# Router logits computed at the end of the merge stage, a scan for the running count, and the slot table built in quarters

## The chip, the cores and the metric

One core of one Trainium2 chip runs the whole kernel. The metric is device time in microseconds (us) of one execution; lower is better.

## The reference

One layer of a hybrid encoder, on x of 2048 tokens x 1024, in float32:

```python
proj = x @ w_in                       # q, k, v of both mixers and the gates
oa   = swa_sink_attention(...)        # 8 heads of 64, window of two 64-token chunks
ob   = diff_attention(...)            # 4 heads, block-causal, then RMSNorm per head
ga, gb = split(sigmoid(gpre + b_gate))
mix = (ga * (oa @ w_proj_a) + gb * (ob @ w_proj_b)) @ w_out
x1  = layer_norm(ALPHA * x + mix)
# mixture of experts: best group of 4, then the best 2 of its 8 experts
glog = x1 @ w_group + b_group         # 4 logits a token
elog = x1 @ w_router + b_router       # 32 logits a token, the chosen group's 8 are kept
eid, wts = top 2 of softmax(elog of the group), scaled by the group's probability
order = argsort(eid)                  # the tokens, sorted by expert
ys  = silu(xs @ gate) * (xs @ up) @ down, expert by expert
out = layer_norm(ALPHA * x1 + scattered sum of wts * ys)
```

## The kernel before, in words

P is 128; the 2048 tokens are NT = 16 tiles of 128 rows. The program is a row of phases (project, diff attention, window attention, merge, route, expert, final). Each phase has a block with one instruction stream per engine, ordered by semaphores alone, and ends with a barrier of all engines. A float32 product is made in three passes of TensorE (PE) from a high part, which ScalarE (ACT) rounds, and a low part, which VectorE (DVE) makes by subtraction.

**Merge** (`merge_phase`, L1368). For each tile PE turns (transposes) `oin` (oa and ob), multiplies by w_proj_a and w_proj_b into the PSUM tiles `psa` and `psb`, turns the gated sum `pa` into `pt`, and multiplies it by w_out into `psw` (L1468 to L1470, 48 matmuls). The order of the work is written out by hand in `step(t, k, u)`: in step t the products of tile t run beside the w_out product of tile t - 1 and the layer norm of tile t - 2. `norm` (L1597) is DVE's: y from `psw`, statistics, a root on ACT, and the scaling; GpSimd (POOL) multiplies by gamma and adds beta, but for the last tile, where DVE does both (L1615, L1617). ACT issues the stores of y to `x1` and to `acc` (L1538, L1539) and at the end waits for them. In the last steps PE has only tile 15's turning and its w_out product left; `psw` is one buffer, so that product waits for `y_done` of tile 14.

**Route** (`route_phase`, L1644). SyncE (SP) loads the router's weights and the 16 tiles of `x1` into four buffers `xin`, and then the 12 slices of expert 0's weights into `rw_raw`. Per tile PE turns the rows (L1767) into one half of `pt`, ACT makes `th` (L1832), DVE makes `tl` (L1869); every fourth tile PE makes the logits of four tiles in 15 matmuls (L1777, L1781), ACT copies them (L1826), PE folds the two halves (L1791) and DVE adds the bias into `lg` (L1863). PE's order is written out by `turn`, `folds`, `logits_of`: a batch's logits come after the turning of the next batch. Then DVE works down one chain, each step `link`ed to the one before by the semaphore `chain`: group and expert choices (L1892 to L1907), the one-hot `o1`, `o2` (L1909), their sum `both` (L1911), its running sum over the tiles in 16 adds (L1913); PE counts with `tri` and `ones` in float32 (L1805 to L1807); DVE does the pair weights (L1919 to L1927), the counts and slots (L1930 to L1947). Last it inverts the permutation: `here` (L1952) and `rows` (L1957) are one-hot comparisons, the four `values` are `here` times the tile (POOL, L1751), times the lane and the low weight (ACT, L1844, L1846) and times the high weight (DVE, L1958), and PE multiplies `rows` by `values` into `table` (L1814, 32 matmuls), from which `weight` and `idx` are read (L1962 to L1969).

**Expert** (`expert_phase`) starts when `idx` stands: ACT and DVE split expert 0's weights (L2170, L2227), POOL gathers the first rows, and PE works through the experts; **final** does the last layer norm.

Of the kernel before, what the change touches and what calls it, by code (L numbers as in the profile page):

```python
# [21 lines left out]
P = 128  # L22
SEQ = 2048
# [78 lines left out]
def f(ap):  # L102

    return ap.bitcast(F32)
# [419 lines left out]
def window_attention_phase(nc, sinks, ident, qk_hi, qk_lo, v_hi, v_lo, oa, w_slices, w_hi, w_lo):  # L524
# [14 lines left out]
    with Phase(nc, "a") as ph:  # L539
# [18 lines left out]
        mask_f = ph.sb("mask_f", [P, P + 2 * M])  # L558
# [93 lines left out]
        def _(pool):  # L652
# [3 lines left out]
            nc.gpsimd.memset(mask_f[:], 0.0).then_inc(mask_step, 1)  # L656
# [134 lines left out]
        def _(dve):  # L791
            dve.wait_ge(mask_step, 10)
            nc.vector.tensor_copy(mask[:], mask_f[:]).then_inc(mask_step, 1)
# [574 lines left out]
def merge_phase(nc, ident, w_hi, w_lo, oa, ob, gates, x, subln_g, ln_g, ln_b, x1, acc):  # L1368
# [4 lines left out]
    KA, KB = A_Q // P, B_V // P  # L1373
    with Phase(nc, "m") as ph:
# [15 lines left out]
        sd, rs = ph.sb("sd", [P, 1]), ph.sb("rs", [P, 1])  # L1390
        pt = ph.ps("pt", [P, D])
# [11 lines left out]
        out_step, stored = ph.sem("out_step"), ph.sems("stored", 2)  # L1403
        block = ph.block()

# [15 lines left out]
        def _(sp):  # L1421
# [31 lines left out]
            for src, dst in ((ln_g, gam), (ln_b, bet)):  # L1453
                sp.dma_start(dst[:], src.to_broadcast([P, D])).then_inc(vec_in, 16)
            over_steps(sp, step)

        @block.tensor
        def _(pe):
# [5 lines left out]
            def product(out, hi, lo, ks, w0, done):  # L1464
                for k in ks:
                    for j in range(D // BANK):
                        js, at, kw = slice(j * BANK, (j + 1) * BANK), slice(k * P, (k + 1) * P), w0 + k
                        nc.tensor.matmul(out[:, js], hi[:, at], w_hi[:, kw, js], start=(k == ks[0]), stop=False)  # L1468
                        nc.tensor.matmul(out[:, js], lo[:, at], w_hi[:, kw, js], start=False, stop=False)
                        last = nc.tensor.matmul(out[:, js], hi[:, at], w_lo[:, kw, js], start=False, stop=(k == ks[-1]))  # L1470
                last.then_inc(done, 1)

            def step(t, k, u):
# [9 lines left out]
                if is_tile(t):  # L1483
# [15 lines left out]
                if is_tile(t - 1):  # L1499
# [9 lines left out]
            over_steps(pe, step)  # L1509

        @block.scalar
        def _(act):
# [12 lines left out]
            def step(t, k, u):  # L1525
# [10 lines left out]
                if is_tile(t - 2):  # L1536
                    act.wait_ge(affine, t - 1)
                    act.dma_start(x1[bass.ts(t - 2, P), :], y[:, u, :]).then_inc(stored[u], 16)  # L1538
                    act.dma_start(acc[bass.ts(t - 2, P), :], y[:, u, :]).then_inc(stored[u], 16)  # L1539

# [5 lines left out]
            over_steps(act, step)  # L1546
            for u in range(2):
                act.wait_ge(stored[u], 32 * (NT // 2 + 1))

        @block.gpsimd  # L1550
        def _(pool):
            nc.gpsimd.memset(eps[:], EPS).then_inc(vec_step, 1)
            nc.gpsimd.memset(eps_x[:], EPS / (ALPHA * ALPHA)).then_inc(vec_step, 1)
            pool.wait_ge(vec_in, 32)
# [14 lines left out]
        def _(dve):  # L1569
# [27 lines left out]
            def norm(t, k, u):  # L1597
# [10 lines left out]
                nc.vector.bn_aggr(mv[:], st[:]).then_inc(var_done, 1)  # L1608
                dve.wait_ge(sd_done, t + 1)
# [833 lines left out]
```

## Time and profile before

| | us |
|---|---|
| median of 3 runs | 2854.07 |
| lowest and highest | 2850.42, 2859.87 |
| the profiled execution | 2856.11 |
| its span | 2854.4 |
| last matmul of the merge ends | 1767.6 |
| first instruction of route | 1778.85 |
| last logits read by DVE | 1831.28 |
| `idx` written | 1870.70 |

| engine | busy us | share of the span |
|---|---|---|
| PE | 2605.3 | 91% |
| DVE | 1629.1 | 57% |
| ACT | 1193.0 | 42% |
| POOL | 530.9 | 19% |

Times inside the execution count from the start of its span. The span and the execution's time differ by 1.7 us that lie around it. The shares are means over stages with different limits; the change touches only the stretch from about 1751 to 1871 us, in which PE's share is far below its mean.

### The profile page before, as it was taken

How to read it: one execution, taken by the hardware profiler on the slowest of the kernel's cores; microseconds unless marked ns; L12 is line 12 of the kernel's file. 1: busy time of each engine (PE TensorE's matmuls, PEld its weight loads, DVE VectorE, ACT ScalarE, POOL GpSimd, SP SyncE). 2: the span in 40 equal slices, each digit the busy share in tenths (PEclk: the TensorE clock that was granted, in tenths of full speed). 3: DMA queues.
4: the chain of work that ended last, by engine and by line, in shares of the span. 5: the costliest groups of instructions: out<-in, count | busy, mean ns of one | idle time of the engine just before them, and what ended most of it. 6: DMA issues, size and time to landing. Idle time of an engine off the chain costs nothing. (4 is left out here: it accounts for less than half of the span.)

```text
span 2854.4 us, 45509 instructions
## 1 busy us (share of the span) xinstructions
PE 2605.3 (91%) x14634; PEld 2245.1 (79%) x14635; DVE 1629.1 (57%) x3067; ACT 1193.0 (42%) x2016; POOL 530.9 (19%) x538
## 2 busy tenths in 40 slices
PE   6999996999999999899799997579999999999990
PEld 5888885788888888799588885468888888888880
DVE  6323322666666666479344443568575577557845
ACT  3111111445444454357111110258575576556846
POOL 0111111101001010135133333022222222222220
PEclk9999998999999999979899998889999999999995
DMA  6344444756575564297333332559687788768946
GB/s 224 122 155 139 136 158 147 215 189 207 168 216 170 178 211 141 94 214 201 134 133 132 132 125 79 211 177 380 233 304 266 235 274 308 233 227 315 379 129 257
DMA packets 262019, 567.45 MB, mean 199 GB/s; under 512 B 27056, under 2 KB 119984, under 8 KB 259872
## 3 DMA queue, kind: packets, MB, share of 16 engines
q1 hardware_dynamic: 169904, 429.45, 44.2%
q0 software_dynamic: 18720, 64.96, 8.8%
q10 hardware_dynamic: 73296, 71.77, 7.4%
q8 instruction: 56, 0.92, 0.1%
q14 instruction: 43, 0.35, 0.0%
HBM read 434.50 MB, written 131.60 MB: 198 GB/s over the span
## 5 line engine op out<-in xcount | busy, mean ns | idle before, releaser
L2227 DVE TENSOR_TENSOR e_wl<-rw_raw,e_wh 128x1024 fp32r<-128x1024 f32 (+1 forms) x384 | 449.6, 1221 | 18.2 <-ACT e_wh L2170 14.4
L2170 ACT ACTIVATE e_wh<-rw_raw 128x1024 fp32r<-128x1024 f32 (+1 forms) x384 | 380.6, 1053 | 4.8 <-PEq L76 4.8
L246 PE MATMUL j_pg<-qkv_w_hi,j_xh 128*128 128x512 f32 (+1 forms) x640 | 243.6, 381 | 10.0 <-DVE qkv_w_lo L416 9.9
L248 PE MATMUL j_pg<-qkv_w_lo,j_xh 128*128 128x512 f32 (+1 forms) x640 | 238.1, 372 | 0.0
L247 PE MATMUL j_pg<-qkv_w_hi,j_xl 128*128 128x512 f32 (+1 forms) x640 | 237.2, 371 | 0.0
L2119 PE MATMUL e_p_up<-e_wh,e_xh 128*128 128x256 f32 (+1 forms) x784 | 225.8, 288 | 0.0
L2121 PE MATMUL e_p_up<-e_wl,e_xh 128*128 128x256 f32 (+1 forms) x784 | 222.0, 283 | 0.0
L2120 PE MATMUL e_p_up<-e_wh,e_xl 128*128 128x256 f32 (+1 forms) x784 | 222.0, 283 | 0.0
L1136 PE MATMUL b_pg<-b_g_wh,b_g_xh 128*128 128x512 f32 x512 | 208.2, 407 | 0.7 <-DVE b_g_out L1323 0.7
L1136 PE MATMUL b_pg<-b_g_wl,b_g_xh 128*128 128x512 f32 x512 | 204.7, 400 | 0.0
L1193 ACT ACTIVATE b_th<-b_t 128x512 fp32r<-128x512 f32 (+3 forms) x160 | 85.4, 534 | 285.0 <-PE b_t L1121 276.3
L1136 PE MATMUL b_pg<-b_g_wh,b_g_xl 128*128 128x512 f32 x512 | 203.1, 397 | 0.0
L1267 DVE TENSOR_SCALAR_CACHE_REDUCE b_sc<-b_s 128x512 f32<-128x512 f32 (+3 forms) x320 | 179.3, 606 | 30.4 <-PE b_s L1108 18.6
L2131 PE MATMUL e_py<-e_wh,e_hh 128*128 128x512 f32 x392 | 166.9, 426 | 0.5
L1308 DVE TENSOR_TENSOR b_tl<-b_t,b_th 128x512 fp32r<-128x512 f32 (+3 forms) x160 | 97.6, 610 | 118.8 <-ACT b_th L1193 118.8
L445 DVE TENSOR_TENSOR j_by_cos<-j_pg,qkv_cos 128x512 f32<-128x512 f32 x64 | 37.7, 589 | 216.4 <-DMA v_lo<-j_staged 145.7
L2119 PE MATMUL e_p_gate<-e_wh,e_xh 128*128 (+1 forms) x392 | 157.2, 401 | 1.3 <-issue 1.3
L1186 ACT ACTIVATE b_sc<-b_sc,b_nb 128x128 f32<-128x128 f32 (+15 forms) x128 | 153.1, 1196 | 6.9 <-DVE b_nb L1278 6.9
L2133 PE MATMUL e_py<-e_wl,e_hh 128*128 128x512 f32 x392 | 154.8, 395 | 0.0
L2132 PE MATMUL e_py<-e_wh,e_hl 128*128 128x512 f32 x392 | 153.9, 393 | 0.0
L2120 PE MATMUL e_p_gate<-e_wh,e_xl 128*128 (+1 forms) x392 | 153.9, 392 | 0.0
L2121 PE MATMUL e_p_gate<-e_wl,e_xh 128*128 (+1 forms) x392 | 153.8, 392 | 0.0
(333 smaller groups left out, 6634.4 us busy)
## 6 DMA issues: line engine op xcount, KB each, us to landing
rw_raw<-w_gate_up SPq DMA_DIRECT2D x256, 512.0 KB, 7.4
rw_raw<-w_down SPq DMA_DIRECT2D x128, 512.0 KB, 9.4
b_g_xh<-xt_hi SPq DMA_DIRECT2D x64, 512.0 KB, 3.7
b_g_xl<-xt_lo SPq DMA_DIRECT2D x64, 512.0 KB, 4.8
gates<-b_g_out ACTq DMA_DIRECT2D x64, 256.0 KB, 5.3
m_gt<-gates SPq DMA_DIRECT2D x16, 1024.0 KB, 8.2
qk_hi<-j_staged ACTq DMA_DIRECT2D x16, 832.0 KB, 4.5
qk_lo<-j_staged ACTq DMA_DIRECT2D x16, 832.0 KB, 7.0
```

What stands on the lines that cost most here:

```text
L246: nc.tensor.matmul(out, xh[:, u, ks], w_hi[:, k, cs], start=(k == 0), stop=False)
L247: nc.tensor.matmul(out, xl[:, u, ks], w_hi[:, k, cs], start=False, stop=False)
L248: last = nc.tensor.matmul(out, xh[:, u, ks], w_lo[:, k, cs], start=False, stop=(k == KD - 1))
L1136: last = nc.tensor.matmul(pg[:], x_side, w_side, start=(q == 0), stop=(q == PASSES - 1))
L1267: nc.vector.tensor_scalar(sc[u][:, m, ks], bank[n % 4][:, 0:ks.stop - ks.start], 1.0, NEG, ALU.mult, ALU.max, accum_out=mx[:, u, m, g:g + ...
L2119: nc.tensor.matmul(out[:, 0:js.stop - js.start], xh[:, at], hi, start=(k == 0), stop=False)
L2120: nc.tensor.matmul(out[:, 0:js.stop - js.start], xl[:, at], hi, start=False, stop=False)
L2121: last = nc.tensor.matmul(out[:, 0:js.stop - js.start], xh[:, at], lo, start=False, stop=(k == KD - 1))
L2131: nc.tensor.matmul(py[:, js], hh[:, at], wh[:, n, js], start=(k == 0), stop=False)
L2133: last = nc.tensor.matmul(py[:, js], hh[:, at], wl[:, n, js], start=False, stop=(k == KF - 1))
L2170: nc.scalar.activation(wh[:, slot(e, s), :], raw[:, s:s + 1, :], ACT.Copy).then_inc(w_hi, 1)
L2227: nc.vector.tensor_tensor(wl[:, slot(e, s), :], raw[:, s:s + 1, :], f(wh[:, slot(e, s), :]), ALU.subtract).then_inc(w_lo, 1)
```

## The change

1. The logits move from the route phase to the end of the merge phase. The landing buffers are `oin` and `gt` (six rows), the turned rows lie in `psa`, `psb` and `pt` in turn, the high and low parts in the first slices of `w_hi` and `w_lo` (w_proj_a's and w_proj_b's place), the copied logits in `pa`. Tiles 0 to 13 are read back from `x1`; 14 and 15 are taken from `y`. Rows 0 and 1 are turned before tile 15's w_out product, row 2 in its middle, the rest after it. SP issues the last two stores instead of ACT. The router's weights are loaded at the merge's start and split in its step 1.
2. In route, the 16 adds become one scan over (expert, tile), which restarts at each expert (`same` is 0 at tile 0); `tri` is shifted by -1 to take the own tile off again; both matmuls go in one pass (float32r), after the column totals; o1 and o2 are made behind the scan. SP loads expert 0's weights first.
3. The table has three values (token, high weight, low weight) instead of four, POOL makes none, and comparison, multiplication and matmuls go by quarters (8 tiles each).
4. `mask_f` of the window attention lies in `raw`.

The core of the diff:

```diff
@@ merge_phase, SP, after over_steps(sp, step)
+            def reload(r):
+                if r < 2:
+                    sp.wait_ge(ab_turned, NT - 1 + r)
+                elif r < len(land):
+                    sp.wait_ge(gated_b, NT - 1 + (r - 2) // 2)
+                else:
+                    sp.wait_ge(r_turned, r - len(land) + 1)
+                sp.wait_ge(stored[r % 2], 32 * (r // 2 + 2))
+                sp.dma_start(land[r % len(land)], x1[bass.ts(r, P), :]).then_inc(landed[r % len(land)], 16)
...
+            for r in range(8):
+                reload(r)
+            store(NT - 2)
+            for r in range(8, FROM_DRAM):
+                reload(r)
+            store(NT - 1)
@@ PE
+                if r < 2:
+                    pe.wait_ge(gated_b if r else gated_a, NT)
+                elif r > 2:
+                    pe.wait_ge(r_lo, r - 2)
+                for c in range(KD):
+                    last = nc.tensor.transpose(buf[:, c * P:(c + 1) * P], src[:, c * P:(c + 1) * P], ident[:])
...
+            def logits_of(i):
+                w = i % 2
+                pe.wait_ge(r_lo, B * i + B)
...
+                if isinstance(t, int) and t == NT:
+                    turn_row(0)
+                    turn_row(1)
...
+                if isinstance(t, int) and t == NT:
+                    pe.wait_ge(y_done, t - 1)
+                    part(psw, mh, ml, range(0, KD // 2), KA + KB, 0, KD - 1)
+                    turn_row(2)
+                    part(psw, mh, ml, range(KD // 2, KD), KA + KB, 0, KD - 1).then_inc(w_done, 1)
...
+            for r in range(3, 6):
+                turn_row(r)
+            logits_of(0)
+            for i in range(1, NBATCH):
+                for r in range(4 * i + 2, min(4 * i + 6, NT) if i < NBATCH - 1 else NT):
+                    if r == 4 * i + 4:
+                        folds(i - 1)
+                        logits_of(i)
+                    turn_row(r)
+            folds(NBATCH - 2)
+            logits_of(NBATCH - 1)
+            folds(NBATCH - 1)
@@ DVE, in norm, between the statistics and the root's reciprocal
+                if isinstance(t, int) and t == NT - 1:
+                    low_row(3)
@@ route_phase, POOL
-                nc.gpsimd.tensor_tensor(values[:, c, :, 0, :], here[:, c], tile_f[:].unsqueeze(2).to_broadcast([P, NT, SLOTS]),
-                                        ALU.mult).then_inc(tiled, 1)
@@ PE
+            nc.tensor.matmul(pc[:], ones_r[:], upto[:, :, NT - 1], start=True, stop=True).then_inc(product, 1)
+            nc.tensor.matmul(pp[:].rearrange("p e t -> p (e t)"), tri_r[:], both[:].rearrange("p e t -> p (e t)"), start=True, stop=False)
+            nc.tensor.matmul(pp[:].rearrange("p e t -> p (e t)"), ones_r[:], upto[:].rearrange("p e t -> p (e t)"), start=False, stop=True).then_inc(product, 1)
@@ DVE
+            link(tt(either[:], sel1[:], sel2[:], ALU.add))
+            link(tt(both[:].rearrange("p (g e) t -> p t g e", g=NG), either[:].unsqueeze(2).to_broadcast([P, NT, NG, EPG]), gate4, ALU.mult))
+            nc.vector.tensor_tensor_scan(upto[:].rearrange("p e t -> p (e t)"), same[:].rearrange("p e t -> p (e t)"),
+                                         f(both[:]).rearrange("p e t -> p (e t)"), 0.0, ALU.mult, ALU.add).then_inc(counted, 1)
...
-            for t in range(NT):
-                ins = tt(before[:, t + 1, :], before[:, t, :], both[:, t].rearrange("p g e -> p (g e)"), ALU.add)
...
-            link(tt(place[:], pp[:], base[:].unsqueeze(1).to_broadcast([P, NT, NE]), ALU.add))
+            dve.wait_ge(product, 2)
+            link(tt(place[:], pp[:].rearrange("p e t -> p t e"), base[:].unsqueeze(1).to_broadcast([P, NT, NE]), ALU.add))
...
+            for c, ts_of in QUARTERS:
+                n = ts_of.stop - ts_of.start
+                tt(rows[:, c, ts_of], ...)
+                dve.wait_ge(in_tile, c + 1)
+                tt(values[:, c, ts_of, 0, :], here[:, c, ts_of], token_f[:, ts_of].unsqueeze(2).to_broadcast([P, n, SLOTS]), ALU.mult)
+                tt(values[:, c, ts_of, 1, :], here[:, c, ts_of], f(pair_hi[:, c, ts_of]).unsqueeze(2).to_broadcast([P, n, SLOTS]),
+                   ALU.mult).then_inc(valued, 1)
```

How the order moves, first on PE at the merge's last tile. Before, tile 15's turning is followed at once by its w_out product:

```order
L1470 MATMUL m_psw<-mw_w_lo,m_mh 128x512
L1461 MATMUL m_pt<-ident,m_pa 128x128 x8
L1468 MATMUL m_psw<-mw_w_hi,m_mh 128x512
L1469 MATMUL m_psw<-mw_w_hi,m_ml 128x512
L1470 MATMUL m_psw<-mw_w_lo,m_mh 128x512
```

and in the changed kernel:

```order
L1520 MATMUL m_psw<-mw_w_lo,m_mh 128x512
L1511 MATMUL m_pt<-ident,m_pa 128x128 x8
L1543 MATMUL m_psa<-ident,m_oin 128x128 x8
L1543 MATMUL m_psb<-ident,m_oin 128x128 x8
L1518 MATMUL m_psw<-mw_w_hi,m_mh 128x512
L1519 MATMUL m_psw<-mw_w_hi,m_ml 128x512
L1520 MATMUL m_psw<-mw_w_lo,m_mh 128x512
```

The turnings of rows 0 and 1 (L1543) stand between the two.

DVE at the end of the merge, from tile 15's statistics on. Before:

```order
L1608 BN_AGGR m_mv<-m_st 128x2
L1610 RECIPROCAL m_rs<-m_sd 128x1
L1615 SCALAR_TENSOR_TENSOR m_y<-m_y,m_mv,m_gam 128x1024
L1617 SCALAR_TENSOR_TENSOR m_y<-m_y,m_rs,m_bet 128x1024
L72 UNCONDITIONAL_BRANCH
```

and in the changed kernel, where L1778 makes a row's low part and L1783 reads logits:

```order
L1760 BN_AGGR m_mv<-m_st 128x2
L1778 TENSOR_TENSOR mw_w_lo<-m_psa,mw_w_hi 128x8x128
L1764 RECIPROCAL m_rs<-m_sd 128x1
L1769 SCALAR_TENSOR_TENSOR m_y<-m_y,m_mv,m_gam 128x1024
L1771 SCALAR_TENSOR_TENSOR m_y<-m_y,m_rs,m_bet 128x1024
L1778 TENSOR_TENSOR mw_w_lo<-m_psb,mw_w_hi 128x8x128
L1778 TENSOR_TENSOR mw_w_lo<-m_pt,mw_w_hi 128x8x128
L1778 TENSOR_TENSOR mw_w_lo<-m_psa,mw_w_hi 128x8x128
L1778 TENSOR_TENSOR mw_w_lo<-m_psb,mw_w_hi 128x8x128
L1783 TENSOR_TENSOR lg<-m_psw,m_br 128x144
```

Row 3 lies inside the last norm, rows 4 to 15 and the four reads behind it.

## Rows read from the trace of the kernel before

**Rows 1.** Stretches: length, busy us of PE, PEld, DVE, ACT, POOL, granted clock, DMA.

```profile
1755.00:1759.00 4.00, 4.00 (x11) 3.17 (x12) 2.22 (x5) 0.29 (x1) 1.15 (x1) 0.60 0.02 4
1768.00:1785.00 17.00, 0.00 (x0) 0.00 (x0) 5.98 (x12) 0.74 (x2) 2.54 (x12) 0.61 0.39 107
1789.00:1799.00 10.00, 5.80 (x44) 4.55 (x43) 7.16 (x6) 5.78 (x6) 0.00 (x0) 1.00 0.87 283
...
1831.00:1833.00 2.00, 0.00 (x0) 0.00 (x0) 1.76 (x9) 0.09 (x1) 0.00 (x0) 1.00 0.03 12
...
1849.00:1864.00 15.00, 0.00 (x0) 0.00 (x0) 14.40 (x20) 6.93 (x23) 5.81 (x2) 0.50 0.00 0
```

**Rows 2.** Timeline of the merge's end: start us, length us, engine.

```profile
1754.86 0.77 PE L1468 MATMUL m_psw<-mw_w_hi,m_mh 128*128 128x512 f32 x1 [3.59 <-DVE m_y L1602]
...
1766.08 0.39 PE L1468 MATMUL m_psw<-mw_w_hi,m_mh 128*128 128x512 f32 x1
1766.76 0.39 PE L1468 MATMUL m_psw<-mw_w_hi,m_mh 128*128 128x512 f32 x1
...
1767.64 1.23 DVE L1602 SCALAR_TENSOR_TENSOR m_y<-m_psw,m_xin 128x1024 f32<-128x1024 f32 x1 [9.87 <-PE m_psw L1470]
...
1772.43 1.28 DVE L1617 SCALAR_TENSOR_TENSOR m_y<-m_y,m_rs,m_bet 128x1024 f32<-128x1024 f32 x1
```

**Rows 3.** Timeline of route's logits: a row's steps, and the last batch.

```profile
1804.43 1.94 ACT L1832 ACTIVATE r_th<-r_pt 128x1024 fp32r<-128x1024 f32 x2 [0.28 <-PE r_pt L1767]
1805.49 2.36 DVE L1869 TENSOR_TENSOR r_tl<-r_pt,r_th 128x1024 fp32r<-128x1024 f32 x2 [3.33 <-ACT r_th L1832]
...
1809.70 0.43 PE L1777 MATMUL r_plt<-r_th,r_wr_hl 128*72 128x512 f32 x1
...
1813.44 1.91 PE L1767 MATMUL r_pt<-ident,r_xin 128*128 128x128 f32 x16
...
1829.20 0.59 ACT L1826 ACTIVATE r_lt<-r_plt 72x512 f32<-72x512 f32 x1 [4.89 <-PE r_plt L1777]
...
1830.97 0.31 DVE L1863 TENSOR_TENSOR r_lg<-r_pl,r_br 128x144 f32<-128x144 f32 x1 [5.18 <-PE r_pl L1791]
```

**Rows 4.** DVE's chain in route, up to the slots.

```profile
1833.66 1.05 DVE L1903 TENSOR_REDUCE r_el<-r_wide 128x128 f32<-128x512 f32 x1
...
1840.59 3.58 DVE L1913 TENSOR_TENSOR r_before<-r_before,r_both 128x32 f32<-128x32 f32 x16
...
1848.31 0.19 DVE L1930 TENSOR_SCALAR r_cnt_f<-r_pc 128x32 f32<-128x32 f32 x1 [2.36 <-PE r_pc L1807]
...
1849.39 0.22 DVE L1935 TENSOR_TENSOR_SCAN r_incl<-r_ones,r_tiles 128x32 f32<-128x32 f32 x1
...
1850.31 0.69 DVE L1940 TENSOR_TENSOR r_place<-r_pp,r_base 128x512 f32<-128x512 f32 x1
```

**Rows 5.** Timeline of the table and of the hand-over to the experts.

```profile
1857.09 4.02 DVE L1957 TENSOR_TENSOR r_th<-r_count_f,r_slot_row 128x2048 fp32r<-128x2048 f32 x1
...
1863.87 2.28 DVE L1957 TENSOR_TENSOR r_th<-r_count_f,r_slot_row 128x2048 fp32r<-128x2048 f32 x1
1864.00 5.58 PE L1814 MATMUL r_pt<-r_tl,r_th 128*128 128x256 f32 x32 [15.73 <-DVE r_tl L1958]
1866.07 1.21 DVE L1958 TENSOR_TENSOR r_tl<-r_xin,r_pair_hi 128x1024 fp32r<-128x1024 f32 x1
1869.63 0.23 DVE L1962 COPY weight<-r_pt 128x64 f32<-128x64 f32 x1 [2.34 <-PE r_pt L1814]
...
1870.42 0.28 DVE L1969 SCALAR_TENSOR_TENSOR idx<-r_empty,r_spare_lane,r_token 128x64 int32<-128x64 f32 x1
1871.65 5.79 ACT L2170 ACTIVATE e_wh<-rw_raw 128x1024 fp32r<-128x1024 f32 x6 [4.76 <-PEq L76]
```

**Rows 6.** The transfers: expert 0's first load, time to landing of `r_xin`.

```profile
1809.97 5.48 SPq L2409 DMA_DIRECT2D rw_raw<-w_gate_up  x8
...
DMA to landing us min/median/max: 3.2/4.5/7.3
```

More of the change, by code:

```diff
@@ L1462, in turn, with part @@
                 last.then_inc(done, 1)
-            def product(out, hi, lo, ks, w0, done):
+            def part(out, hi, lo, ks, w0, first, end):
                 for k in ks:
@@ L1471, in product, with turn_row @@
-                last.then_inc(done, 1)
+                        last = nc.tensor.matmul(out[:, js], hi[:, at], w_lo[:, kw, js], start=False, stop=(k == end))
+                return last
+            def product(out, hi, lo, ks, w0, done):
+                part(out, hi, lo, ks, w0, ks[0], ks[-1]).then_inc(done, 1)
+            def turn_row(r):
+                buf = turned_in[r % 3]
+                if r < FROM_DRAM:
+                    pe.wait_ge(landed[r % len(land)], 16 * (r // len(land) + 1))
+                    src = land[r % len(land)]
+                else:
+                    if r == NT - 1:
+                        pe.wait_ge(last_affine, 1)
+                    else:
+                        pe.wait_ge(affine, r + 1)
+                    src = y[:, r % 2, :]
+                if r < 2:
[4 more added lines that the diff above has]
+                    last = nc.tensor.transpose(buf[:, c * P:(c + 1) * P], src[:, c * P:(c + 1) * P], ident[:])
+                last.then_inc(r_turned, 1)
@@ new lines, in logits_of, with high @@
+            def logits_of(i):
+                w = i % 2
+                pe.wait_ge(r_lo, B * i + B)
+                if i == 0:
+                    pe.wait_ge(wr_split, 2)
+                    pe.wait_ge(y_done, NT)
+                else:
+                    pe.wait_ge(lt_done, i)
+                for c in range(KD):
+                    def high():
+                        return nc.tensor.matmul(plt, wr_hl[:, c, :], th[:, w, c, :], start=(c == 0), stop=(c == KD - 1))
+                    if c == 0:
+                        high()
+                    nc.tensor.matmul(plt[0:NL, :], wr_hl[:, c, 0:NL], tl[:, w, c, :], start=False, stop=False)
+                    if c:
+                        last = high()
+                last.then_inc(r_product, 1)
@@ L1473, in step, with folds @@
+            def folds(i):
+                pe.wait_ge(lt_done, i + 1)
+                if i:
+                    pe.wait_ge(logits, i)
+                else:
+                    pe.wait_ge(fold_step, 3)
+                for v in range(B):
+                    last = nc.tensor.matmul(pl[:, v, :], lt[:, i % 2, v * P:(v + 1) * P], fold[:], start=True, stop=True)
+                last.then_inc(folded, 1)
             def step(t, k, u):
@@ L1697, in route_phase @@
         found, split_pair = ph.sem("found"), ph.sem("split_pair")
         block = ph.block()
[L1704 to L1707 removed]
+        QUARTERS = [(c, slice(n * NT // 2, (n + 1) * NT // 2)) for c in range(2) for n in range(2)]
@@ L1770, in logits_of @@
-            def logits_of(i, w):
-                pe.wait_ge(t_lo, B * i + B + 2)
-                pe.wait_ge(lt_done, i + 1)
-                for c in range(KD):
-                    def high():
-                        return nc.tensor.matmul(plt[:], wr_hl[:, c, :], th[:, w, c, :], start=(c == 0), stop=(c == KD - 1))
-                    if c == 0:
-                        high()
-                    nc.tensor.matmul(plt[0:NL, :], wr_hl[:, c, 0:NL], tl[:, w, c, :], start=False, stop=False)
-                    if c:
-                        last = high()
-                last.then_inc(product, 1)
@@ L1804, in _ @@
[L1804 to L1813 removed]
+            pe.wait_ge(one_pass, 2)
```

295 lines of the change are left out of this document (138 added, 157 removed).

## The prediction

> **What bounds the kernel now.** I read the page first: PE is busy 91% of the span, so only a stretch in which PE waits can give time back at little cost. The busy time by stretches shows where that is: for 17 us around the end of the merge PE does nothing, in route's logits it is busy 5.80 of 10 us, and from 1849 to 1864 us it rests while DVE is busy 14.40 of 15 us [rows 1]. The timeline then gives the chain from the merge's last product to `idx`. The product waits 3.59 us for `psw`, runs at a clock of 0.60 at first, and DVE's norm follows until 1773.7 [rows 1, 2]. The last logits are read at 1831.28 [rows 3]. DVE alone goes on [rows 4], then DVE and PE make the table, and the first expert work follows `idx` by 0.95 us (1870.70 to 1871.65) [rows 5]. Nothing else of the kernel can begin before that, so what leaves this chain leaves the time. After it PE is the bound as before, and the change leaves that part alone.
>
> **A: the logits in the merge's tail.** What it removes: the wait for the stores, the barrier, the loads' latency and the start of route, during which no logits are made.
>
> - Last product. Rows 0 and 1 are turned (0.95 us each, 1.91 for two [rows 3]) in the 3.59 us in which PE waited, at no cost, since y_done of tile 14 still ends later. The product is 16 groups of three matmuls 0.68 apart, 10.9 us at the full clock [rows 2], plus row 2's turning, 0.95. Begun at 1754.86, it ends at 1766.7 instead of 1767.6: I take the clock to stay up, since only 1.7 us stay idle. If it falls as before (0.60), the end is 1768.5.
> - Norm of tile 15. It takes 6.1 us (1767.64 to 1773.71 [rows 2]); row 3's low part (1.2 us) comes in, of which the wait for the root hides 0.4. It ends at 1773.6: nothing gained, nothing lost, and row 3 is done.
> - First logits: PE begins them at row 3's low part, about 1771.1, and they end at 1775.0 (15 matmuls took 3.75 us from 1809.70 to the next turning [rows 3], and the last ends 0.15 later). Rows 6 and 7 are turned behind them and ACT makes row 7's high part by 1777.9 (0.97 a row [rows 3]) and DVE its low part by 1779.3. Logits 1 begin at 1779.4.
> - Batches 2 and 3. The order has the four turnings directly ahead of their own logits, so nothing covers the last row: first row 0.95, the high part 1.1 later (behind ACT's copy), then four low parts at 1.18 (2.36 for two [rows 3]), 0.1 to PE: 6.85 us, and 3.75 us of logits, 10.6 a batch. DVE sets it; in route's order the turnings of the next batch covered that row. Logits 3 begin at 1779.4 + 2 x 10.6 = 1800.6 and end at 1804.5.
> - The end: from the last matmul to the last read took 2.1 us (ACT's copy at 1829.20, read done at 1831.28 [rows 3]), so 1806.6. Then the barrier, for which I take the 0.95 us of the next boundary, and 0.2 for the first `iota`. The stores of tile 15 are long done by then. The chain starts 24.7 - 1.15 = **23.5 us** earlier.
>
> The reloads are hidden: six rows have buffers, a reload has six turnings' time (some 16 us) and lands in 3.2 to 7.3 [rows 6]. SP is held at the store of tile 14 until POOL has added beta, during the last product; reload 8 behind it is first needed near 1783. The early part of the merge gets four small loads, 0.9 us of ACT and DVE, in steps where both idle 10 us: nothing. `mask_f` costs nothing: `raw` is filled after the first scores, which wait for the mask.
>
> **B: counting.** Gone are the 16 adds, 3.5 us, and DVE's wait for PE, 2.36 [rows 4], since o1, o2 and the pair weights now stand between; the sum `both` of 0.69 goes as well. New are `either` (128 elements, 0.3 by the rows for 32 and 512), `both` with a strided output, the scan, and three casts that ran at route's start (0.45 together). For `both` I take the strided reduction's 1.05 rather than 0.69 (same 512 elements [rows 4]), and the same 0.36 more for `place`, which now reads PSUM in strides; the ends are 0 and 0.36 for each. The scan: 0.22 us for 32 elements beside 0.19 for a plain operation of that size, so 0.03 x 16 = 0.5 on top of 0.69 [rows 4], 1.2; the ends are 0.69 and 1.4. Sum: -3.5 - 2.36 - 0.69 + 0.3 + 1.05 + 1.2 + 0.45 + 0.36 = **-3.2**.
>
> The two rows are 0.03 us apart at 32 elements, which could as well be a fixed cost and make the scan 0.7. Here a page speaks against the cheap reading: the Trainium skill, "DVE: opcode table, instruction layouts, handler registers and perf-mode slots", section "Datapath and trigger behaviour", says that the built-in scan runs at half throughput. By it B would be -3.2, by the fixed-cost reading -3.7. On strides, the Trainium skill, "SBUF — State Buffer", section "Door 1: The DMA port swizzle", says that accesses pay for each new 16-byte line, and 8-byte in PSUM; by that the PSUM read could cost more than the 0.36 of the SBUF row, which no row here shows.
>
> **C: the table.** Before: `rows` and `values` on DVE took 10.2 us (1857.09 to 1867.28), of which POOL's work beside them cost some 3.4: the same comparison took 4.02 with POOL busy and 2.28 without [rows 5]. Now a quarter is 1.17 (half of 2.28) and two multiplications of 512 elements, 0.62 each back to back: 2.4, four of them 9.65. **-0.5**. ACT has 8 of its 0.24 us multiplications a quarter, 1.95: hidden. Behind the last DVE instruction PE had 16 matmuls of 256 columns, 2.35 us to the read [rows 5]; now 8 of 192, 1.3 us at the clock of 0.50 that stretch shows [rows 1], plus 0.2: **-0.85**. One DVE step of the read goes: **-0.15**.
>
> **Sum.** -23.5 - 3.2 - 0.5 - 0.85 - 0.15 = -28.2 us. The profiled execution took 2856.1, so 2827.9. It lies 2.0 us over the median of the three runs; for a median I forecast 2826, which is 1.0% less.
>
> **Rivals.**
>
> 1. *The clock falls in the tail.* PE now waits some 2 us for DVE in each batch, and at the merge's end a gap of 3.59 us brought 0.60 for the next 4 us [rows 1, 2]. Against it: with PE busy 58% in route's first turnings the clock stayed at 1.00 [rows 1]. If it fell in all four batches, 15 matmuls would cost 0.2 more each, 3 us a batch, and the exposed turning 0.7: 15 us, so 2841.
> 2. *B and C give nothing* (strides, the scan and the quarters' fixed costs eat it): 23.5 remain, 2830.5. It lies inside the range.
> 3. *Expert 0's weights become the bound.* They were first issued at 1809.97 and the transfers were over by about 1831 [rows 1, 6], 21 us; the first issue is now near 1808, so they stand by 1829, and `idx` is due at 1842.5. The cover is 13 us. Only with twice the duration would the gain shrink, at worst to nothing: 2854. Against it: nothing else loads then.
> 4. *The reloads bind: slower.* Rows 6 to 13 are read back in two rounds, each waiting for a buffer and then for a landing. Beyond 16 us of landing each round costs what lies over it. To eat 28 us and 9 more, a landing would have to take 34 us; the longest of these loads took 7.3 [rows 6]. 2865 if so.
>
> **How the numbers follow.** Forecast with its bounds: 0.85; rival 1: 0.07; rival 2 is part of the forecast's lower gain; rival 3: 0.04; rival 4: 0.02; 0.02 for what I have not seen. The range: a batch of 10.2 to 12 us (-1, +3), the boundary 0.5 to 3 (-0.5, +2), the product's clock (+2), B (-1, +1.5) and the runs' own spread, 2850.4 to 2859.9 (-3, +4). Taken together 2819 to 2834. A measurement of this kernel tells 0.3%, 8.6 us, from no change. Faster by more than that holds for the forecast, rival 1 and 2: 0.93; same 0.04; slower 0.03.
>
> **What would show it right or wrong.** The last read of logits near 1806.6, a batch every 10.6 us, DVE without a gap in the four low parts, the last product ending before 1767 at a clock near 1.0; DVE's scan at 1.2 and no wait for PE at the counts; comparisons of 1.2 us with POOL idle; the read of the table 1.5 us behind the last multiplication; `idx` near 1842.5. A landing over 10 us, or a batch over 12 us, would make the forecast wrong, and so would an expert phase that grows.

## The result, and the profile after

| | us |
|---|---|
| before, median of 4 runs | 2853.02 (2850.42 to 2859.87) |
| the changed kernel, median of 4 runs | 2826.82 (2825.18 to 2831.76) |
| ratio, 95% interval | 0.9908 (0.9895 to 0.9922) |
| the profiled execution, its span | 2831.76, 2830.0 |

By the medians the change is faster by 26.2 us, 0.9%; a median of 2826 was forecast. The profile shows where that comes from. "Turning" is a transpose on PE, and "the tail" is the merge's last stretch, in which PE, ACT and DVE now make the logits. The stretches first, with the columns of [rows 1]:

```profile
1755.00:1759.00 4.00, 4.00 (x13) 3.15 (x12) 3.44 (x6) 2.12 (x3) 1.96 (x1) 0.60 0.22 87
...
1785.00:1795.00 10.00, 7.72 (x45) 5.40 (x44) 4.92 (x5) 3.88 (x4) 0.00 (x0) 0.86 0.00 0
...
1795.00:1807.00 12.00, 9.73 (x56) 6.93 (x55) 4.93 (x5) 4.47 (x5) 0.00 (x0) 0.83 0.01 1
...
1826.00:1828.00 2.00, 0.00 (x0) 0.00 (x0) 1.79 (x8) 0.00 (x0) 0.00 (x0) 0.50 1.06 352
...
1831.00:1846.00 15.00, 8.09 (x32) 7.12 (x32) 12.82 (x22) 7.74 (x32) 0.00 (x0) 0.50 0.00 1
```

PE now works where it had rested, from 1785 to 1807, but in both of these stretches, and at the start of tile 15's product, the granted clock is a mean between 1.2 and 2.4 GHz (0.86, 0.83, 0.60) where I had taken 1.00. (Before, the start of the product was at 0.60 too.) No transfer of note runs from 1785 to 1807. The clock stands at 0.50 while the table is made. PE in the tail, with the wait ahead of each row in brackets, as in [rows 2]:

```profile
1754.05 0.47 PE L1518 MATMUL m_psw<-mw_w_hi,m_mh 128*128 128x512 f32 x1 [1.85 <-DVE m_y L1754]
...
1754.86 0.63 PE L1518 MATMUL m_psw<-mw_w_hi,m_mh 128*128 128x512 f32 x1
...
1790.88 0.45 PE L1557 MATMUL m_psw<-mw_w_hi,m_wr_hl 128*72 128x512 f32 x1 [1.56 <-DVE mw_w_lo L1778]
...
1792.77 0.63 PE L1557 MATMUL m_psw<-mw_w_hi,m_wr_hl 128*72 128x512 f32 x1
...
1796.20 1.03 PE L1543 MATMUL m_psa<-ident,m_oin 128*128 128x128 f32 x8
...
1803.14 0.70 PE L1557 MATMUL m_psw<-mw_w_hi,m_wr_hl 128*72 128x512 f32 x1 [1.56 <-DVE mw_w_lo L1778]
```

After a rest of 1.85 us the product's matmuls go from 0.39 us to 0.63, and after one of 1.56 the third batch of logits does the same. From that batch's first matmul to the first turning behind it pass 5.32 us; the second batch, with its matmuls at 0.39 to 0.40, took 3.77. PE has no wait for a DMA between the merge's last product and the last logits. DVE beside it:

```profile
1767.81 1.23 DVE L1754 SCALAR_TENSOR_TENSOR m_y<-m_psw,m_xin 128x1024 f32<-128x1024 f32 x1 [3.21 <-PE m_psw L1520]
...
1786.07 1.23 DVE L1778 TENSOR_TENSOR mw_w_lo<-m_pt,mw_w_hi 128x1024 fp32r<-128x1024 f32 x1 [5.74 <-ACT mw_w_hi L1673]
1787.21 1.22 DVE L1778 TENSOR_TENSOR mw_w_lo<-m_psa,mw_w_hi 128x1024 fp32r<-128x1024 f32 x1
1788.34 1.22 DVE L1778 TENSOR_TENSOR mw_w_lo<-m_psb,mw_w_hi 128x1024 fp32r<-128x1024 f32 x1
1789.60 1.23 DVE L1778 TENSOR_TENSOR mw_w_lo<-m_pt,mw_w_hi 128x1024 fp32r<-128x1024 f32 x1
1790.74 0.30 DVE L1783 TENSOR_TENSOR lg<-m_psw,m_br 128x144 f32<-128x144 f32 x1
...
1810.13 0.31 DVE L1783 TENSOR_TENSOR lg<-m_psw,m_br 128x144 f32<-128x144 f32 x1 [6.83 <-PE m_psw L1573]
1811.70 0.28 DVE L1944 CAST r_desc<-r_desc_i 128x8 f32<-128x8 int32 x1 [1.26 <-POOL r_desc_i L1881]
1812.02 0.22 DVE L1948 TENSOR_REDUCE r_gm<-lg 128x16 f32<-128x64 f32 x1
```

The four low parts run without a gap, 1.13 to 1.26 apart. The batches follow each other by 10.71 and 12.26 us (1780.17, 1790.88, 1803.14): DVE and the full-clock logits give the first, the slow matmuls the second. A batch is 16 matmuls in the code and in the trace, not the 15 that I counted; the time of a batch was read from the trace and stands. The last logits are read at 1810.44. Behind that, the constants of route are POOL's, and DVE's first reduction starts 1.58 us after the read (0.23 before, 1831.28 to 1831.51). DVE's chain, against [rows 4, 5]:

```profile
1818.92 0.28 DVE L1964 TENSOR_TENSOR r_either<-r_sel 128x128 f32<-128x128 f32 x1
1819.24 1.01 DVE L1965 TENSOR_TENSOR r_both<-r_either,r_gsel 128x512 fp32r<-128x512 f32 x1
1820.29 1.23 DVE L1967 TENSOR_TENSOR_SCAN r_upto<-r_same,r_both 128x512 fp32r<-128x512 f32 x1
...
1825.03 0.18 DVE L1989 TENSOR_SCALAR r_cnt_f<-r_pc 128x32 f32<-128x32 f32 x1
...
1827.04 0.69 DVE L2000 TENSOR_TENSOR r_place<-r_pp,r_base 128x512 f32<-128x512 f32 x1
...
1833.69 1.22 DVE L2015 TENSOR_TENSOR r_rows<-r_count_f,r_slot_row 128x1024 fp32r<-128x1024 f32 x1
1834.82 0.69 DVE L2018 TENSOR_TENSOR r_values<-r_here,r_token_f 128x512 fp32r<-128x512 f32 x1
1835.42 0.69 DVE L2019 TENSOR_TENSOR r_values<-r_here,r_pair_hi 128x512 fp32r<-128x512 f32 x1
...
1842.44 0.68 DVE L2019 TENSOR_TENSOR r_values<-r_here,r_pair_hi 128x512 fp32r<-128x512 f32 x1
1845.24 0.23 DVE L2024 COPY weight<-r_table 128x64 f32<-128x64 f32 x1 [2.11 <-PE r_table L1909]
```

The scan takes 1.23 us, the strided `both` 1.01. `place` reads PSUM in strides in the same 0.69 us as the contiguous one [rows 4]. No wait for PE stands at the counts: the column totals were ready before they were wanted. A quarter's comparison takes 1.22. PE and POOL, up to the first expert's first product:

```profile
1821.66 0.37 PE L1901 MATMUL r_pc<-r_upto,r_ones_r 128*128 128x32 f32 x1 [11.56 <-DVE r_upto L1967]
...
1843.18 2.02 PE L1909 MATMUL r_table<-r_values,r_rows 128*128 128x192 f32 x8 [0.31 <-DVE r_values L2019]
...
1848.05 2.10 POOL L2106 DMA_INDIRECT e_xg<-x,e_idx_in  x1 [0.93 <-POOL e_idx_in L2103]
...
1859.74 0.79 PE L2180 MATMUL e_p_gate<-e_wh,e_xh 128*128 x1 [1.26 <-issue]
```

The counts' first matmul needs 0.37 us and starts behind the scan. Eight table matmuls take 2.02 us, 0.25 each, at the clock of 0.50. The gather's instruction took 2.10 us on POOL here (1.04 before), and PE's first product comes 13.69 us behind `idx` (12.05 before).

### The profile page after: what moved, and what is told of

Its sections match the earlier page's. It is cut to its first block and busy times, and to the rows that moved or that the text cites. A ratio compares the mean times of both kernels' runs of the same rounds, so it can differ in the third digit from the quotient of the medians.

```text
span 2830.0 us, 45509 instructions
## 1 busy us (share of the span) xinstructions
PE 2608.0 (92%) x14631; PEld 2248.3 (79%) x14632; DVE 1625.0 (57%) x3059; ACT 1190.8 (42%) x2016; POOL 527.2 (19%) x538
```

## The experiments

The profiled executions reach the merge's end up to 12 us apart (1744.4 in t1, 1756.3 in t8), and t7, which is the change once more, reaches it 4.7 us before the change's first profile, so the cause lies in earlier phases. Whether the small loads and splits that the change adds ahead of that point cost anything can't be told: its eleven profiles reach it at 1744.4 to 1756.3, the one of before at 1753.5. So I measure each profile from M, where DVE starts to read `psw` for tile 14 (1753.50 before, 1752.69 after). The parts: **product** from M to the same read for tile 15; **logits** on to the end of their last read; **gap** to the first reduction; **counts** to `cnt_f`; **table** to the first read of the table; **to idx** on to the end of `idx`'s writing. All are in us, one profiled execution each.

| kernel | product | logits | gap | counts | table | to idx | M to idx |
|---|---|---|---|---|---|---|---|
| before | 14.14 | 63.64 | 0.23 | 16.80 | 21.32 | 1.07 | 117.20 |
| the change | 15.12 | 42.63 | 1.58 | 13.01 | 20.21 | 0.81 | 93.36 |
| t1 logits only | 13.50 | 45.57 | 3.75 | 16.78 | 22.21 | 1.07 | 102.88 |
| t2 logits, counts | 15.06 | 44.12 | 1.57 | 13.07 | 21.79 | 1.07 | 96.68 |
| t3 PE kept on | 13.47 | 39.78 | 1.58 | 13.00 | 20.21 | 0.81 | 88.85 |
| t4 rows ahead | 13.50 | 36.40 | 1.58 | 13.01 | 20.21 | 0.81 | 85.51 |
| t5 table warm | 13.47 | 41.31 | 1.57 | 13.01 | 20.20 | 0.81 | 90.37 |
| t6 halves | 15.08 | 42.61 | 1.57 | 13.00 | 21.50 | 0.81 | 94.57 |
| t7 the change again | 15.07 | 42.60 | 1.57 | 13.00 | 20.20 | 0.81 | 93.25 |
| t8 all together | 13.46 | 35.00 | 1.57 | 13.00 | 20.21 | 0.81 | 84.05 |
| t9 rows ahead, kept on | 13.46 | 34.96 | 1.58 | 13.01 | 20.21 | 0.81 | 84.03 |
| t10 t4 again | 13.46 | 36.55 | 1.58 | 13.02 | 20.21 | 0.81 | 85.63 |

The times, with the kernel before measured beside them (t1 to t4 ran on one chip, t5 to t8 on a second, t9 and t10 on a third):

| kernel | time | kernel before | ratio, interval |
|---|---|---|---|
| t1 | 2834.78 (2832.83 to 2842.10) | 2853.03 | 0.9942 (0.9919 to 0.9965) |
| t2 | 2826.73 (2822.45 to 2834.13) | 2853.03 | 0.9900 (0.9881 to 0.9920) |
| t3 | 2825.66 (2825.15 to 2826.60) | 2853.03 | 0.9901 (0.9883 to 0.9919) |
| t4 | 2821.43 (2819.39 to 2825.54) | 2853.03 | 0.9892 (0.9872 to 0.9911) |
| t5, t6, t7 | 2830.04, 2831.78, 2825.91, one run each | 2855.66 | |
| t8 | 2822.16 (2820.65 to 2826.66) | 2855.66 | 0.9879 (0.9863 to 0.9896) |
| t9 | 2821.90 (2817.98 to 2831.92) | 2856.51 | 0.9891 (0.9873 to 0.9910) |
| t10 | 2820.32 (2815.46 to 2825.19) | 2856.51 | 0.9877 (0.9860 to 0.9894) |

### t1: the logits alone

The merge is the changed one; route's counting and table are those of before.

```diff
-            nc.vector.tensor_tensor_scan(upto[:].rearrange("p e t -> p (e t)"), same[:].rearrange("p e t -> p (e t)"),
-                                         f(both[:]).rearrange("p e t -> p (e t)"), 0.0, ALU.mult, ALU.add).then_inc(counted, 1)
...
+            for t in range(NT):
+                ins = tt(before[:, t + 1, :], before[:, t, :], both[:, t].rearrange("p g e -> p (g e)"), ALU.add)
...
-            for c, ts_of in QUARTERS:
+            for c in range(2):
```

> Part A alone: the logits are made in the merge's tail as in the change, but the counting (16 adds, float32 matmuls) and the table (four values, POOL makes one) are those of before. My theory, from the two traces: A gives 18.7 us up to the first step of the chain, B 3.8 and C with the read 1.4, so in this kernel DVE's counts begin 16.8 us after the first reduction as before (13.0 in the change), the table takes 21.3 to 21.6 us from there to its read, and the whole is 5 us slower than the change: about 2832 us. Rival: B and C are worth nothing once A moves the work (what they save returns as a wait at the experts' start): then the time is that of the change, 2827.

Measured: 18.3 us less than before and 8 more than t2 and the change, where 5 more than the change was expected; to `idx` it takes 9.5 us more than the change. DVE's rows on the counts and the table, and below them two stretches of before:

```profile
1824.02 0.19 DVE L2002 TENSOR_SCALAR r_cnt_f<-r_pc 128x32 f32<-128x32 f32 x1 [2.37 <-PE r_pc L1916]
...
1846.23 0.23 DVE L2034 COPY weight<-r_pt 128x64 f32<-128x64 f32 x1 [3.22 <-PE r_pt L1923]
```

```profile
1864.00:1865.00 1.00, 1.00 (x4) 1.00 (x5) 1.00 (x1) 1.00 (x6) 0.00 (x0) 0.50 0.00 0
...
1868.00:1869.00 1.00, 1.00 (x11) 1.00 (x10) 0.00 (x0) 0.00 (x0) 0.00 (x0) 1.00 0.00 0
```

The wait for the counts is back with 2.37 us, and the comparison of `rows` takes 4.02 (at 1832.81) beside POOL, as before [rows 4, 5]. Two numbers are new. The gap is 3.75 us and not 1.58, because this route's DVE still waits for all of POOL's constants, the last of them a 0.94 us fill:

```profile
1805.72 0.94 POOL L1905 MEMSET r_zero<- 128x1024 f32 x1
```

So 2.2 us of what I had booked under A are earned by the rewritten start of route, not by the move of the logits. And the table is read 3.22 us behind the last multiplication, where before, with the same 32 matmuls, it was 2.35. What differs is when the clock rises in the middle of them: their starts go from 0.21 us apart to 0.12 at 1867.5 before, for the last 16, and here at 1845.2, for the last 7. The last batch of logits was slow here too, 14 of its 16 matmuls.

### t2: the logits and the counts, the table as before

```diff
-        QUARTERS = [(c, slice(n * NT // 2, (n + 1) * NT // 2)) for c in range(2) for n in range(2)]
+        QUARTERS = [(c, slice(0, NT)) for c in range(2)]
...
+            pool.wait_ge(in_tile, 1)
+            for c in range(2):
+                nc.gpsimd.tensor_tensor(values[:, c, :, 0, :], here[:, c], tile_f[:].unsqueeze(2).to_broadcast([P, NT, SLOTS]),
+                                        ALU.mult).then_inc(tiled, 1)
```

> A and B as in the change, the table as before (whole columns of 16 tiles, four values, POOL makes one). Theory: only C is missing, 12.6 us on DVE instead of 11.7, 2.35 us of PE behind it instead of 2.1, one more step in the read: 1.4 us slower than the change by the trace, about 2828. Rival: the weight loads of expert 0, now first in SP's queue, slow DVE in this stretch, then DVE's comparisons beside POOL take over 4.1 us.

Counts take 13.07 us against 16.78 in t1: B is worth 3.7. The table with the read of it takes 22.86 against 21.02 in the change: C is worth 1.8, of which 0.26 lies in the read. Against the kernel before, C came to 1.4: there 16 of the table's matmuls had the full clock and here 11, which makes the wait for the read 2.35 us there and 2.82 here. DVE's comparison beside POOL took 4.03 us, so expert 0's weights, now loaded first, didn't slow it. To `idx` t2 takes 3.3 us more than the change, and the 1.5 beyond C are its slower last batch. In the time the two kernels can't be told apart (2826.73 and 2826.82), and needn't be: that is less than the runs spread.

### t3: PE is kept busy in the tail

Turnings of the identity that nobody reads fill PE's waits ahead of the product and of each batch of logits; all else is the change.

```diff
+            def keep(n):
+                for _ in range(n):
+                    nc.tensor.transpose(psw[:, 0:P], ident[:], ident[:])
...
-                for c in range(KD):
-                    last = nc.tensor.transpose(buf[:, c * P:(c + 1) * P], src[:, c * P:(c + 1) * P], ident[:])
+                for again in range(3 if r == 1 else 1):
+                    for c in range(KD):
+                        last = nc.tensor.transpose(buf[:, c * P:(c + 1) * P], src[:, c * P:(c + 1) * P], ident[:])
...
+                if i == 0:
+                    pe.wait_ge(y_done, NT)
+                    keep(11)
+                else:
+                    pe.wait_ge(lt_done, i)
+                    keep(14)
```

> The change, but PE turns row 1 three times ahead of the last w_out product and turns the identity 11 or 14 times ahead of each batch of logits, so that it hardly rests there (turnings whose result nothing reads). Theory: the clock fell in the change because PE rested (1.85 us ahead of the product, 1.6 us ahead of logits 2 and 3), so here the product takes 11.9 us instead of 13.75, all batches of logits 3.8 us, the last read comes 4 to 5 us earlier, and the time is about 2822. Rival: the clock falls there for another reason than the rest (a turning counts as rest, or it falls at some time whatever PE does): then the granted clock stays at 0.6 after the product's begin, logits 2 and 3 keep 5.2 us, and the time is that of the change or 1 us above.

```profile
1755.00:1759.00 4.00, 4.00 (x19) 3.29 (x19) 3.44 (x6) 2.12 (x3) 1.94 (x1) 1.00 0.38 128
...
1785.00:1795.00 10.00, 9.28 (x66) 7.33 (x66) 4.35 (x5) 3.78 (x6) 0.00 (x0) 1.00 0.01 2
...
1795.00:1803.00 8.00, 7.28 (x51) 5.45 (x49) 4.93 (x5) 2.93 (x4) 0.00 (x0) 1.00 0.00 0
```

These are the stretches that showed 0.60, 0.86 and 0.83 in the change. With 1.00 throughout, the product takes 13.47 us and every batch of logits 3.76; the batches begin 10.69 apart, which is the 10.6 of the prediction. M to `idx` is 88.85, which is 28.35 less than before. In the time the gain over the change is 1.2 us, inside the change's spread, and the 2822 that was expected wasn't reached. The 4.5 us are shown in the profile alone.

### t4 and t10: the rows are turned ahead of the logits

PE, ACT and DVE do two rows of the next batch before the logits of this one, as route's order did.

```diff
+            turn_row(6)
+            turn_row(7)
...
-                for r in range(4 * i + 2, min(4 * i + 6, NT) if i < NBATCH - 1 else NT):
-                    if r == 4 * i + 4:
-                        folds(i - 1)
-                        logits_of(i)
+                folds(i - 1)
+                for r in range(4 * i + 4, min(4 * i + 6, NT)):
+                    turn_row(r)
+                logits_of(i)
+                for r in range(4 * i + 6, min(4 * i + 8, NT)):
                     turn_row(r)
```

> The change, but PE turns the first two rows of the next batch ahead of a batch's logits, and ACT makes their high parts ahead of the copy. Theory: the exposed part of a batch was the wait for the last row's low part (DVE sets the 10.7 to 12.3 us of a batch); with two rows ahead the batch falls to 8.4 us (the sum of PE's own work), PE no longer rests 1.6 us, the clock stays up, and the last read comes 6 to 8 us earlier: about 2820. Rival: ACT or the buffers bind (row 4i+5 waits for the low part of row 4i+2), then a batch stays over 10 us and the gain is under 2 us.

> t4 again, in the same call as t9, for the comparison: 2821 us, 49.9 us in the tail, 4.2 us less where tile 15's product and the last logits run at the full clock than where the clock falls.

```profile
1783.70 1.23 DVE L1781 TENSOR_TENSOR mw_w_lo<-m_psa,mw_w_hi 128x1024 fp32r<-128x1024 f32 x1
1784.84 1.22 DVE L1781 TENSOR_TENSOR mw_w_lo<-m_psb,mw_w_hi 128x1024 fp32r<-128x1024 f32 x1
1789.40 1.23 DVE L1781 TENSOR_TENSOR mw_w_lo<-m_pt,mw_w_hi 128x1024 fp32r<-128x1024 f32 x1 [3.34 <-ACT mw_w_hi L1674]
...
1798.94 0.31 DVE L1786 TENSOR_TENSOR lg<-m_psw,m_br 128x144 f32<-128x144 f32 x1 [6.97 <-PE m_psw L1573]
```

The reads of logits come 8.3 us apart (1775.07, 1783.38, 1791.67). DVE's wait between two pairs of low parts is 3.36 us where the change has 5.74 and 7.29 in its last two batches. From the product to the last read it is 36.40 and 36.55 us, 6 less than the change. The 1.6 us that the product is shorter are not the order's: the clock didn't fall there in these two executions, with the same rest of 1.85 us. The medians, 2821.43 and 2820.32, are the lowest and fit the 2820 expected, but those of t8 and t9 lie within 2 us of them. Behind the first batch PE has nothing to wait for until the last:

```profile
1791.81 0.70 PE L1557 MATMUL m_psw<-mw_w_hi,m_wr_hl 128*72 128x512 f32 x1 [1.81 <-DVE mw_w_lo L1781]
...
1793.16 0.63 PE L1557 MATMUL m_psw<-mw_w_hi,m_wr_hl 128*72 128x512 f32 x1
```

There it rests 1.81 us and goes on at 0.63, in t4 and in t10 alike.

### t5: the table with PE at work before it

104 unread turnings stand between the counts and the table.

```diff
+            for _ in range(104):
+                nc.tensor.transpose(spare[:], ident[:], ident[:])
```

> The change, with PE turning the identity 104 times between the counting and the table (results nobody reads). Question: what sets the 0.25 us of a table matmul, which I had put at 0.16 (192 columns at the low clock). If the clock alone: at the full clock the eight last matmuls take half, 1.0 us instead of 2.0, and the read follows the last multiplication by 1.1 instead of 2.1 us, 1 us off the time. Rival: a fixed cost per matmul (its weight load) that the clock doesn't touch: then 2.0 us stay.

```profile
1836.73 1.12 PE L1913 MATMUL r_table<-r_values,r_rows 128*128 128x192 f32 x8
...
1843.24 2.02 PE L1913 MATMUL r_table<-r_values,r_rows 128*128 128x192 f32 x8 [1.08 <-DVE r_values L2023]
```

PE waits between the quarters' matmuls, and the clock, at 1.00 for the first quarter (8 matmuls in 1.12 us), is back at 0.50 for the last (2.02 us). The read comes 2.12 us behind the last multiplication, as without the turnings: nothing won, where 1 us was expected. That the quarters' matmuls would be faster at the high clock holds, but the quarter that is waited for is the last.

The 192 columns didn't set their duration: at 0.50 these matmuls start 0.21 us apart (the change), and so do those of 256 columns before; at 1.00 it is 0.11 here and 0.12 before. So three values instead of four saved PE next to nothing; what saved it time is that half as many matmuls stand behind the last multiplication. What sets the 0.21, no run here shows.

### t6: the table in halves

```diff
-        QUARTERS = [(c, slice(n * NT // 2, (n + 1) * NT // 2)) for c in range(2) for n in range(2)]
+        QUARTERS = [(c, slice(0, NT)) for c in range(2)]
```

> The change, with the table in two steps of 16 tiles instead of four of 8 (three values, no POOL, all else as in the change). Theory: the quarters are worth what PE has left after DVE's last multiplication: 16 matmuls of 0.25 instead of 8, so the read comes 4.1 us behind it instead of 2.1; against it DVE has 6 instructions less, 0.4 us. Net 1.6 us slower than the change from the slots to idx. Rival: the gain of C comes from POOL's absence alone and the quarters add nothing.

```profile
1843.00 3.73 PE L1909 MATMUL r_table<-r_values,r_rows 128*128 128x192 f32 x16 [0.74 <-DVE r_values L2019]
...
1846.77 0.23 DVE L2024 COPY weight<-r_table 128x64 f32<-128x64 f32 x1 [3.82 <-PE r_table L1909]
```

16 matmuls stand behind the last multiplication, and the read comes 3.82 us after it, 1.7 later than with quarters. DVE's own work is 0.4 shorter with fewer instructions. So the quarters are worth 1.3 us of C's 1.8, and three values instead of four, with POOL out of the way, the other 0.5. The split between the two holds for these executions only: t2's last 11 matmuls had the full clock, and none of t6's.

### t7: the change once more

No edit.

> The change once more, for its profile. Theory: the clock falls in the last product and in the batches of logits in some executions and not in others, with the same rests of PE before them: the product takes either 13.5 or 15.1 us (from the one y to the next) and a batch's 15 matmuls 3.8 or 5.2 us. Rival: the change always shows 15.1 and 3.8, 5.3, 5.2.

It repeats the first profile to 0.1 us in every part, with the clock's fall in the same places, as the rival of the expectation had it. That this isn't so in every execution is shown by t5, whose merge is the same code: there the product and the third batch kept the clock. Also, the gather's instruction took 1.04 us here: PE's first product followed `idx` by 11.97 us. The 13.69 of the first profile is thus no part of the change.

### t8: rows ahead, PE kept on from the merge to the first expert

t4, t3's turnings ahead of the product, the first and the last logits, t5's 104 turnings, and 78, 14 and 12 more while the first expert waits for its rows.

```diff
@@ expert_phase, PE, around the first expert's turning of its rows
+            for _ in range(78):
+                nc.tensor.transpose(px[:, 0:P], ident[:], ident[:])
...
+            for _ in range(14):
+                nc.tensor.transpose(py[:, 0:P], ident[:], ident[:])
```

> Rows ahead of the logits as in the fourth run, PE kept on ahead of the product, logits 0 and logits 3, before the table and while the first rows of expert 0 are gathered. Theory: on top of the fourth run (2821.4) the product keeps the clock (up to 1.6 us), logits 3 too (1.5), the table's end 1.0, and the first expert's matmuls run at 0.23 instead of 0.43 each, 2.6 us: about 2816. Rival: in the first expert ACT and DVE with the split of the weights bind, and the full clock there returns as a wait: then 2819.

```profile
1841.44 10.88 PE L2216 MATMUL e_px<-ident 128*128 128x128 f32 x78 [1.97 <-PEq L76]
...
1842.33 1.04 POOL L2124 DMA_INDIRECT e_xg<-x,e_idx_in  x1 [0.93 <-POOL e_idx_in L2121]
...
1852.16 0.60 PE L2176 MATMUL e_px<-ident,e_xg 128*128 128x128 f32 x4
...
1856.58 0.49 PE L2198 MATMUL e_p_gate<-e_wh,e_xh 128*128 x1 [0.44 <-DVE e_xl L2317]
```

M to `idx` is 84.05 us, the shortest so far. But the 78 turnings were begun at a clock of 0.50 and took 10.88 us, while PE's turning of the gathered rows had followed the gather's issue by 4.4 in t4. It comes here 9.8 behind it, and the first product 16.25 behind `idx` against 11.94: what the tail gave, this took, and 2816 wasn't reached. From the first product on the kernel needed 968.3 us, 2.5 less than t4, with those matmuls 0.23 us apart from the start, so the high clock did gain about what was expected of it in the first expert. The rival isn't what took it: PE was busy 16.56 of the 17 us from 1853 on. A filler has to end before what it fills for arrives.

### t9: t8 without the turnings in route and in the expert phase

What is left beside t4's order:

```diff
+                if i == 0:
+                    pe.wait_ge(y_done, NT)
+                    keep(11)
+                elif i == NBATCH - 1:
+                    pe.wait_ge(lt_done, i)
+                    keep(14)
```

Row 1 is turned three times ahead of the product, as in t3.

> The order of t4 with unread turnings of the identity on PE only where PE would rest in the tail: while it waits for psw ahead of tile 15's product, ahead of the first logits and ahead of the last. Nothing is added in route or in the expert phase. If the clock is what is left to win in the tail, the product of tile 15 takes 13.5 us from read to read and the last batch of logits 3.75 us in every execution, the last read of logits comes 48.5 us behind the start of tile 15's norm's first read of psw for tile 14 (49.9 in t4), and the time is 1 to 3 us below t4's of the same call. If t8's slow first expert had nothing to do with the 104 turnings added there after idx, this kernel too has 16 us from idx to the first expert matmul; by my reading it has 12. The rival: the tail's clock does not reach the end, and the times are equal.

Parts as expected: product 13.46, the last batch at the full clock, 1.6 us less to `idx` than t10, and 11.96 from `idx` to the first product. In the time nothing is to be seen: 2821.9 beside 2820.3 for t10. The runs of t10 spread over 9.7 us and those of t9 over 13.9, so 1.6 us would need many more runs. Of the two I would keep t10, which has no idle work in it.

## Why the prediction was right, and where it wasn't

- **The total.** Forecast 28.2 us, measured 26.2 by the medians. Between the two profiles the span fell by 24.4 us: 0.8 before M, 23.8 from M to `idx` (117.20 to 93.36), +1.6 from `idx` to the first product, which t7 doesn't show, and 1.4 behind it (971.65 to 970.26), where the other profiles lie between 968.3 and 971.2. The rest of the way to 26.2 is where the profiled executions stand among the runs. Nothing here shows that the medians gain anything outside this stretch.
- **A, forecast 23.5 at the first reduction, measured 18.7 from M.** The step that failed is "Begun at 1754.86, it ends at 1766.7 instead of 1767.6: I take the clock to stay up, since only 1.7 us stay idle", and with it the 3.75 us of logits in each of the "Batches 2 and 3". The rest was 1.85 us, and the clock fell: against t3 the product took 1.6 us longer, the third batch 1.6 and the fourth 1.3. That is 4.5 of the 4.8 missed, and t3 gives them back in its profile. The last two batches began 12.26 us apart, over the 12 that I had named as a sign of a wrong forecast. The rest of A stands: turnings at no cost, 10.7 a batch at the full clock, no wait for a reload anywhere.
- **The boundary** cost 1.58 us where I had 1.15, from which the 0.23 that lay there before should have been taken off. That is nearly right only because route's start was rewritten: with the old one it is 3.75 (t1).
- **B, forecast 3.2, measured 3.8.** Of the forecast, 3.55 us lie ahead of `cnt_f`, where the 3.8 were measured; the 0.36 added for the strided read of PSUM by `place` lies behind it and wasn't there. The scan came at 1.23 for 1.2 and `both` at 1.01 for 1.05, and the fixed-cost reading, 0.7 for the scan, is refuted. By the Trainium skill, "DVE: opcode table, instruction layouts, handler registers and perf-mode slots", section "Datapath and trigger behaviour", the built-in scan runs at half throughput, and the trace agrees: 1.23 us against 0.69 for a plain operation on 512 elements.
- **C, forecast 1.5 with the read, measured 1.4; 1.8 against t2.** Two errors met: a matmul of 192 columns took 0.25 us at the clock of 0.50 and not 0.16, so the read came 2.1 behind the last multiplication and not 1.5 (I had worked from the columns, and had set beside it the 2.35 of before, which was mostly at the full clock, as shown at t1); and DVE's part was 0.4 shorter than summed.
- **Rival 1** happened in part. It named four batches at 3 us each and came in two at about half of that: a fall cost 1.3 to 1.6 us and not 3, since only about half of a batch's matmuls were slow and the rest had the full clock again. In t1 and t2 nearly all of the last batch were slow, and it cost 2.8 us more than in t3. It was no case apart, as its chance of 0.07 had it: in each of the six profiles with this merge the clock fell in one to three of the four batches.
- **Rival 2** is refuted by the parts of t1 and t2 (t1's median lies 8 us over t2's), **rival 3** by the trace: expert 0's weights were still coming after 1828, but nothing moved any more from 1831 on, 15 us ahead of `idx`. **Rival 4** has nothing for it: no wait of PE in the tail ends with a DMA, and DMA is all but idle from 1785.

That the forecast hit the median to 1 us is partly luck: to `idx` the sum was 4.4 us too good, and the runs' own spread (9.5 us before, 6.6 after) moved the medians the other way. Of the two profiles that of after stands 5 us over its median where that of before stands 3 over, and the kernel before is 1 us lower with its fourth run.

## What to carry to other kernels

When work moves into a tail where two engines take turns, price it at both levels of TensorE's clock, each short wait by itself, and order it so that the next rows are turned before the products that wait: that gave 4.8 us with the clock kept up in both (39.78 to 34.96 us of logits, t3 and t9), as much as keeping it up by unread work, and takes nothing in return. Judge parts of 1 to 3 us by distances inside the profile from a mark ahead of the change, since the time of this kernel of 2.8 ms differs by 1.5 to 14 us between its four or five runs. Split the last step before a hand-over, so that little work stands behind the last instruction of the engine that is waited for.

## What the runs showed of the hardware

- **The granted clock can fall after rests of 1.5 to 1.9 us, and does not always.** In the same code the product fell after 1.85 us in the change, t2, t6 and t7 and not in t1, t4, t5 and t10. The first batch of logits never did after 1.47 us, the second did in t1 alone, after 1.81; the third stayed up in t5 only, of the executions of that order; the last, after 1.56 to 1.81, always fell. When PE was kept on it never fell in this stretch (t3, t8, t9). Shorter rests can do it as well: in t5's table it fell behind two rests of 0.71 and 1.20 us between the quarters. What in an execution decides it, I didn't find; when the stretch begins is one thing that differs. The Trainium skill, "TensorE: Matmul & The Clock Gate", section "A second HAM failure mode: psum-queue depth-cycling", tells of a kernel in which frequent short rests between groups of matmuls made the clock go up and down; these traces agree with it.
- **A strided read of PSUM by DVE cost nothing:** 0.69 us for 512 elements, as when contiguous, while a reduction of 512 elements from SBUF took 1.06 in strides and 0.69 contiguous. The Trainium skill, "SBUF — State Buffer", section "Door 1: The DMA port swizzle", gives PSUM lines of 8 bytes and says that accesses that aren't contiguous slow matmuls down; this read by DVE shows no such cost.
- **The same gather** held POOL for 1.04 us in ten of the profiles and for 2.10 in two (the change's first and t1), and PE turned its rows 6.7 us behind the issue in those and 4.2 to 5.0 in the others but t8.
